# Two modulation blocks of a scan round share one PSUM bank, one row copy, one product set and one small copy

## What is computed

```python
def modulation(cvec, ada_w, ada_b):
    m = jax.nn.silu(cvec) @ ada_w + ada_b          # 1024 -> 6 x 1024
    return jnp.split(jnp.expand_dims(m, -2), N_MOD, axis=-1)

def modulate(x, g, shift, scale):
    return rmsnorm(x, g) * (1 + scale) + shift
...
        sh_p, sc_p, gt_p, sh2_p, sc2_p, gt2_p = modulation(c_ctx, ada_w[i], ada_b[i])
        sh_s, sc_s, gt_s, sh2_s, sc2_s, gt2_s = modulation(c, ada_w[i], ada_b[i])
...
    def step(S, inp):                              # the scan, one direction
        r_t, w_t, k_t, v_t, a_t, b_t = inp
        sa = jnp.einsum('bhij,bhj->bhi', S, a_t)
        S = (S * w_t[..., None, :] + v_t[..., :, None] * k_t[..., None, :]
             + sa[..., :, None] * b_t[..., None, :])
        return S, jnp.einsum('bhij,bhj->bhi', S, r_t)
```

## Time and profile before

| | |
|---|---|
| median of 3 runs | 1603.58 us (1592.74 to 1609.02) |
| profiled execution | 1589.24 us, its span 1587.4 us |
| TensorE busy in the span | 1325.0 us (83%) |
| VectorE, ScalarE, GpSimd busy | 516.3, 336.1 and 355.7 us |
| mean granted TensorE clock | 0.885 of full speed |
| scan phase, rounds with blocks | about 255 to 559 us of the span |
| rounds without blocks | three, about 559 to 660 us |

### The profile page before, as it was taken

One profiled execution on the slowest core, in us unless ns is written; L12 is line 12 of the kernel. 1 busy time (PEld: TensorE's weight loads), 2 busy tenths in 40 slices (PEclk: granted clock), 3 DMA queues, 4 the chain that ended last, 5 costly groups with the idle time before them and its releaser, 6 DMA issues. The chain is left out here.

```text
span 1587.4 us, 21701 instructions
## 1 busy us (share of the span) xinstructions
PE 1325.0 (83%) x8603; PEld 931.1 (59%) x8603; DVE 516.3 (33%) x1152; ACT 336.1 (21%) x834; POOL 355.7 (22%) x689
## 2 busy tenths in 40 slices
PE   6699986999999988799577898479987884998865
PEld 4356842788788877635444565255675554555534
DVE  1710064465565555362410111130025433111115
ACT  1200161233232221031311111021115312111111
POOL 0000003345444432100023232000007400233300
PEclk8799975899999989689689999779998995999995
DMA  9532043557655424206269977638220152877713
GB/s 328 171 105 80 0 126 116 169 164 224 184 172 162 137 49 137 106 5 243 93 244 394 355 273 245 236 72 171 92 71 1 54 242 88 322 268 248 267 68 119
DMA packets 199764, 262.01 MB, mean 165 GB/s; under 512 B 94128, under 2 KB 155968, under 8 KB 184048
## 3 DMA queue, kind: packets, MB, share of 16 engines
q1 hardware_dynamic: 166048, 222.51, 41.7%
q0 software_dynamic: 17312, 31.51, 5.4%
q10 hardware_dynamic: 16304, 6.61, 2.3%
HBM read 300.27 MB, written 26.34 MB: 206 GB/s over the span
## 5 line engine op out<-in xcount | busy, mean ns | idle before, releaser
L1911 PE MATMUL psum<-ring,slab 128*64 128x256 f32 x896 | 197.0, 402 | 32.6 <-DMA slab<-moe_w,slab 30.3
L1911 PE MATMUL psum<-slab 128*64 128x256 f32 x832 | 179.0, 392 | 0.0
L1911 PEld LDWEIGHTS psum<-ring,slab 128*64 128x64 f32 x896 | 118.7, 146 | 94.9 <-issue 54.4
L1911 PEld LDWEIGHTS psum<-slab 128*64 128x64 f32 x832 | 110.1, 141 | 3.6 <-issue 1.0
L1939 PE MATMUL psum<-ring,ws 128*64 128x512 f32 x224 | 94.1, 595 | 16.9 <-issue 15.3
L2032 DVE TENSOR_TENSOR ws<-ws,psum 128x256 f32<-128x256 f32 (+1 forms) x28 | 17.2, 614 | 241.1 <-PE psum L1911 241.1
L2155 PE MATMUL psum<-slab,ring 128*128 128x384 f32 x256 | 84.8, 495 | 6.0 <-PEq L166 6.0
L1939 PE MATMUL psum<-slab,ws 128*64 128x512 f32 x208 | 87.5, 598 | 1.3 <-issue 1.3
L1972 POOL DMA_INDIRECT y_rows<-slab x28 | 28.3, 1009 | 252.8 <-DVE slab L2042 252.8
L613 PE MATMUL psum<-slab,ring 128*128 128x384 f32 x256 | 82.7, 486 | 0.0
L1237 DVE TENSOR_TENSOR ws<-psum,causal 128x512 f32<-128x512 f32 x96 | 62.9, 685 | 48.6 <-PE psum L933 46.7
(11 more groups left out here) (344 smaller groups left out, 2440.6 us busy)
## 6 DMA issues: line engine op xcount, KB each, us to landing
ring<-moe_w SPq DMA_DIRECT2D x84, 1024.0 KB, 6.9
ring<-ada_w SPq DMA_DIRECT2D x48, 1024.0 KB, 9.2
ws<-inverses SPq DMA_DIRECT2D x48, 256.0 KB, 3.7
slab<-moe_w SPq DMA_DIRECT2D x12, 1024.0 KB, 8.7
ring<-na_w_qkv SPq DMA_DIRECT2D x12, 1024.0 KB, 5.3
slab<-y_rows SPq DMA_DIRECT2D x12, 512.0 KB, 3.8
ring<-rwkv_w_r SPq DMA_DIRECT2D x4, 1024.0 KB, 7.9
ring<-rwkv_w_k SPq DMA_DIRECT2D x4, 1024.0 KB, 5.2
```

The costliest lines, as they stand in the source:

```text
L1911: last = nc.tensor.matmul(k.psum[BT * g:BT * g + BT, h_bank(s, kind), 0:DE], cols_[s % 2][:, c, BT * g:BT * g + BT], w[g][:, c, :], start= ...
```

## The change

Blocks 2m and 2m+1 become one pair m. Both are accumulated into bank 2 (direction 0's), in one group of matmuls per column tile: the silu tile is padded to 34 columns with the vectors in columns 2 and 3, so that a slice from column 2 puts the even block in rows 32c and 32c+1, and a slice from column 0 puts the odd block in rows 32c+2 and 32c+3. One row copy, one select with a 128x4 `sel` (128x16 in all) and one small copy follow. The select stands where the one of the even block stood; the second is gone, and with it direction 1's wait for `sel_ok`. The matmuls of `modulate`, the weight loads from DRAM and their order are the same. The vector's zero padding takes two GpSimd memsets where one stood.

```diff
-    sel = np.zeros((P, 2))
+    sel = np.zeros((P, 4))
...
-        sel[32 * g, 0] = sel[32 * g + 1, 1] = 1.0
+        sel[32 * g + np.arange(4), np.arange(4)] = 1.0
...
-        self.silu_c = sb("silu_c", [P, DC, 32])
-        self.sel = sb("sel", [P, 2])
+        self.silu_c = sb("silu_c", [P, DC, 34])
+        self.sel = sb("sel", [P, 4])
...
-            nc.scalar.activation(k.silu_c[:, :, 0:1], c2[:, :, 1:2], ACT.Silu).then_inc(sig_c, 1)
-            nc.scalar.activation(k.silu_c[:, :, 1:2], c2[:, :, 0:1], ACT.Silu).then_inc(sig_c, 1)
+            nc.scalar.activation(k.silu_c[:, :, 2:3], c2[:, :, 1:2], ACT.Silu).then_inc(sig_c, 1)
+            nc.scalar.activation(k.silu_c[:, :, 3:4], c2[:, :, 0:1], ACT.Silu).then_inc(sig_c, 1)
...
-            nc.gpsimd.memset(k.silu_c[:, :, 2:32], 0.0).then_inc(sig_c, 1)
+            nc.gpsimd.memset(k.silu_c[:, :, 0:2], 0.0).then_inc(sig_c, 1)
+            nc.gpsimd.memset(k.silu_c[:, :, 4:34], 0.0).then_inc(sig_c, 1)
...
-                    last = nc.tensor.matmul(k.psum[32 * g:32 * g + 32, 0, :], k.silu_c[:, c, :], w[:, 512 * g:512 * g + 512],
+                    last = nc.tensor.matmul(k.psum[32 * g:32 * g + 32, 0, :], k.silu_c[:, c, 2:34], w[:, 512 * g:512 * g + 512],
...
-    def blocks(r):
-        return [(n, D2[n % 2]) for n in (2 * r + 2, 2 * r + 3) if n < len(ADA)]
+    MOD_PAIRS = len(ADA) // 2
...
-            def modulate(n, o):
-                for half in range(2):
-                    i = 2 * n + half
-                    pe.wait_ge(k.ada_in[i % 4], 16 * (i // 4 + 1))
-                    w = k.ring[:, ADA_SLOTS[i % 4], :].rearrange("p (c n) -> p c n", c=4)
-                    for c in range(4):
-                        last = nc.tensor.matmul(k.psum[32 * c:32 * c + 32, o.bank + 2, :], k.silu_c[:, 4 * half + c, :], w[:, c, :],
-                                                start=half == 0, stop=half == 1)
-                    last.then_inc(ada_mul, 1)
-            def select(n, o):
-                pe.wait_ge(ada_ok, n + 1)
+            def modulate(m):
+                for n in (2 * m, 2 * m + 1):
+                    to_rows = slice(2, 34) if n % 2 == 0 else slice(0, 32)
+                    for half in range(2):
+                        i = 2 * n + half
+                        pe.wait_ge(k.ada_in[i % 4], 16 * (i // 4 + 1))
+                        w = k.ring[:, ADA_SLOTS[i % 4], :].rearrange("p (c n) -> p c n", c=4)
+                        for c in range(4):
+                            last = nc.tensor.matmul(k.psum[32 * c:32 * c + 32, 2, :], k.silu_c[:, 4 * half + c, to_rows], w[:, c, :],
+                                                    start=i % 4 == 0, stop=i % 4 == 3)
+                        last.then_inc(ada_mul, 1)
+            def select(m):
+                pe.wait_ge(ada_ok, m + 1)
...
-                    last = nc.tensor.matmul(k.psum[:, o.bank + 2, 2 * t:2 * t + 2], o.rows[:, P * t:P * t + P], k.sel[:],
+                    last = nc.tensor.matmul(k.psum[:, 2, 4 * t:4 * t + 4], D2[0].rows[:, P * t:P * t + P], k.sel[:],
...
-            for n, o in blocks(-1):
-                modulate(n, o)
-            for n, o in blocks(-1):
-                select(n, o)
-            for n, o in blocks(0):
-                pe.wait_ge(sel_ok, n - 1)
-                modulate(n, o)
+            modulate(0)
+            select(0)
+            pe.wait_ge(sel_ok, 1)
+            modulate(1)
...
-                    for n, o in blocks(r)[d:d + 1]:
-                        select(n, o)
+                    if d == 0 and r + 1 < MOD_PAIRS:
+                        select(r + 1)
...
-                    for n, o in blocks(r)[d:d + 1]:
-                        pe.wait_ge(sel_ok, n + 1)
+                    if d == 0 and r + 1 < MOD_PAIRS:
+                        pe.wait_ge(sel_ok, r + 2)
...
-                for n, o in blocks(r + 1):
-                    modulate(n, o)
+                if r + 2 < MOD_PAIRS:
+                    modulate(r + 2)
...
-            def rows_copy(r):
-                for n, o in blocks(r):
-                    act.wait_ge(ada_mul, 2 * n + 2)
-                    if n < 2:
-                        act.wait_ge(band_out[n], 32)
-                    nc.scalar.copy(o.rows, k.psum[:, o.bank + 2, :]).then_inc(ada_ok, 1)
-            def mod_copy(r):
-                for n, o in blocks(r):
-                    layer, j = ADA[n]
-                    act.wait_ge(sel_done, n + 1)
-                    nc.scalar.copy(k.mod[:, 48 * layer + 4 * j:48 * layer + 4 * j + 4, :],
-                                   k.psum[:, o.bank + 2, 0:8].rearrange("p (t s) -> p t s", t=4)).then_inc(sel_ok, 1)
-            rows_copy(-1)
-            mod_copy(-1)
+            def rows_copy(m):
+                act.wait_ge(ada_mul, 4 * m + 4)
+                if m == 0:
+                    act.wait_ge(band_out[0], 32)
+                nc.scalar.copy(D2[0].rows, k.psum[:, 2, :]).then_inc(ada_ok, 1)
+            def mod_copy(m):
+                layer, j = ADA[2 * m]
+                act.wait_ge(sel_done, m + 1)
+                nc.scalar.copy(k.mod[:, 48 * layer + 4 * j:48 * layer + 4 * j + 8, :].rearrange("p (b t) s -> p b t s", b=2),
+                               k.psum[:, 2, 0:16].rearrange("p (t b s) -> p b t s", t=4, b=2)).then_inc(sel_ok, 1)
+            rows_copy(0)
+            mod_copy(0)
...
-                rows_copy(r)
+                if r + 1 < MOD_PAIRS:
+                    rows_copy(r + 1)
...
-                mod_copy(r)
+                if r + 1 < MOD_PAIRS:
+                    mod_copy(r + 1)
...
-            dve.wait_ge(sel_ok, len(ADA))
+            dve.wait_ge(sel_ok, MOD_PAIRS)
...

```

## The result

| | before | changed |
|---|---|---|
| median of 20 runs | 1587.79 us | 1599.74 us |
| lowest, highest | 1573.93, 1609.02 | 1584.10, 1609.14 |
| profiled execution, its span | 1589.24, 1587.4 | 1584.10, 1582.3 |
| rounds 1 to 3, one round, clock 1.00 | 30.35 | 30.62 |
| rounds 4 to 7, one round, clock 1.00 | 31.59 | 31.85 |

The changed kernel takes 1.0074 of the time of before, 95% interval 1.0041 to 1.0108: some 12 us slower. With 17 more runs the median of before came down from 1603.58 to 1587.79, so the absolute forecast of 1604.3 lies near the measured 1599.74 by two errors that partly cancel: a starting point that was 16 us too high, and a loss of 12 us where 0.7 were forecast. The ratios in this text leave out runs more than 1.5% above a kernel's fastest, and as falls of the clock make just such runs here, medians over all runs stand beside them.

A forecast was written before the change was run, and what follows sets the result against it. In rounds 1 to 8 TensorE and VectorE were taken to reach the bands together, TensorE binding by 0.04 us only. +2.5 - 1.7 - 0.04 = +0.7 us on 1603.58 gave 1604.3 us, range 1588 to 1614.

The forecast's parts named there:

- wrong if the granted clock in them is below 1.00: Sign against the prediction: TensorE's granted clock in rounds 1 to 8 of the profile after falls below 1.00.
- The select is worth 0.04 us in rounds 1 to 8, as VectorE arrives with it: Ahead of the bands: 1.32 us leaves TensorE, but VectorE's chain lets the bands start only 0.04 us earlier.
- TensorE is the bound after all: Rival, rounds 0 to 8: bands do not wait for VectorE, 13.0 us gained, 1590.6 us; chance 0.07.
- GpSimd's key scaling starts at 408.98 and holds line 1207: Rounds 1 to 7: earlier GpSimd reads hold VectorE, bands 0.35 us later each round, +2.5 us in all.
- The other order at the shared reads: Rival, rounds 1 to 7: GpSimd comes 0.07 us earlier, holds lines 1205 and 1207; +4.9 us, 1608.5; chance 0.15.
- Round 0 gains 1.7 us: Round 0, TensorE at half clock: removing the second select gains 1.7 us, bounds 1.32 and 2.44.
- The clock falls in the new gap: Rival: TensorE idles 1.5 us ahead of the bands, clock falls, 4.56 us each; four falls give 1622.5 us; chance 0.10.
- The starting point: The median before, 1603.58 us, to which the forecast change of +0.7 us was added.

The follow-up runs named there:

- without the stay: Changed kernel with GpSimd's key scaling also waiting for first_ok of direction 1, so VectorE is not held behind GpSimd: 0.9990 of before, median 1585.63 us.
- thin filler: Changed kernel plus four idle 4-column products between the second set of pairs and the bands, rounds 1 to 8: 0.9996 on five runs, median of all 1601.75 us.
- longer idle select: Changed kernel plus an idle second select in the old place, five products long instead of four in rounds 1 to 8: 1.0053 of before, median 1590.17 us.

## Why the prediction was right and where it was wrong

It forecast no change that can be told (0.85 for within 1%). The change was 0.74%, and the time lies in the range, but the size was wrong, 12 us for 0.7, and the main part of the 12 us comes by a way that the prediction had as a rival of 0.10. That the time lies in the range is luck. The range was built around a starting point 16 us too high; built in the same way around the median of 20 runs, 1587.79, it would have been 1572 to 1598, and 1599.74 lies outside. By the prediction's own sign ("wrong if the granted clock in them is below 1.00") it failed: in rounds 1 and 5 the clock was 0.90 and 0.78.

- *The select is worth 0.04 us in rounds 1 to 8, as VectorE arrives with it*. Right: without the stay the bands start at 5.67 (forecast: 410.50 on round 4's scale, which is 5.67), and the levels 0.15 earlier than before. So the rival *TensorE is the bound after all* is out.
- *GpSimd's key scaling starts at 408.98 and holds line 1207*. Right: measured 4.14 into the round, 408.97 on that scale; the held instruction took 0.84 us (forecast 0.81), the bands came at 6.09 (forecast 6.06). The round grew by 0.26, not 0.35, since the first half of the bands was now loaded in 0.55 instead of 0.63 and the levels followed 1.54 behind the bands' start instead of 1.66. The other order at the shared reads (0.15) did not occur in any round. The rule cited from the Trainium skill ("SBUF — State Buffer", section "Who interferes with whom") holds in both directions here: GpSimd's pairs of instructions also took 1.44 and 1.37 us instead of 1.19.
- *Round 0 gains 1.7 us*. Mis-sized: rounds 0 of the nine profiles with the short layout took 32.4 to 32.9 us against 35.5 in the profile before, so 2.6 to 3.1 less. In the changed kernel's profile the bands of round 0 started 7.83 into the round and the levels at 9.48, 1.65 later and so at full clock: it had risen by then, where I had left its rise at its old moment. In one profile of the old layout the clock was high from the start of round 0 and the round took 30.44; then there was nothing to gain.
- *The clock falls in the new gap*: the rival of 0.10, and the step that failed. I had its place and its sign and three things wrong. The price: 4.56 us from round 9, where a fall at the bands cost 7.6, because the clock stayed low for some 17 us, over the two levels. The chance: round 10, which kept its clock in one execution, I took as evidence that such a stretch is mostly harmless; another profile then had 42.89 us in that same round. And what was removed: I counted the select as work that the gap takes away. It is not that. The thin filler put the same work back and the falls stayed. What fits the runs, but is argued and not shown, is that the change joined thin stretches (a gap or four products of few columns, then the bands with their waits, then levels of 64 columns) that the pairs had kept apart, and moved the rounds to other moments. With a second select in its old place the falls come behind it, pairs follow, and the clock is back ahead of the levels.
- *The starting point.* The median of three runs, 1603.58, was 16 us above that of 20. The prediction allowed 5 us for this.

Not settled: how much of the falls is due to the length of the thin stretch and how much to the moments at which the rounds come; why the longer idle select, with neither gap nor stay, cost 0.5%; why most falls at the bands last through the two levels and cost 7.6 us while one cost 3.0; and 2 to 3 of the 12 us.

## What to carry to other kernels

Removing small products from a full TensorE is worth only what the other engine's chain leaves, and here that was 0.04 us a round; read it from a round that lacks them already. Ask what a TensorE stretch gets thinner by it, and judge the clock by many runs' mean granted clock, not by one profile in which a suspect round happens to have kept it. Where a wait is unavoidable, some wide products that nobody reads can be cheaper than nothing: with them and one wait for GpSimd the kernel came to 0.988 to 0.996 of before. Try it and measure many runs, as the fall can also move to the next gap.

## What the runs showed of the hardware

- Weight loads with products of 4 columns and with products of 128 columns take the same time (0.97 us for four fp32 products), but with the former the granted clock fell in three of rounds 1 to 8 (in two of them at the bands), with the latter in none; the mean clock of 12 runs was 0.880 and 0.891. In round 10 six products of 128 columns ahead of the bands did not keep it: 32.28, 32.45 and 42.89 us in three of four profiles, 27.74 in the fourth.
- A fall of the clock cost 1.7, 3.0, 4.6, 7.6 or over 13 us in otherwise equal rounds; round 9, with the same instructions in nine of the kernels, took 27.69 to 41.16 us.
- A VectorE instruction with two SBUF inputs that met a GpSimd instruction with two took 0.84 us instead of 0.42, and slowed GpSimd's by 0.18 to 0.25 us a pair; VectorE instructions that read PSUM and one SBUF input (1.42 and 2.60 us) were not changed by the same neighbour.
- One program's runs on one chip spread from 1574 to 1609 us, and the mean granted clock explains most of it (correlation -0.90).
